# Expert tables with a 512-column moving operand, and the 8 sample tokens' expert rows fetched by indirect DMA

## The reference, cut to what matters

```python
q = (xf @ wq).reshape(n, 8, 2, 128)
s = einsum('nhpd,hpkd->nhpk', q, keys)            # 128 scores for each of 8 heads x 2 halves
top_s, top_i = top_k(s, 16)
best_s, pos = top_k(all 16 x 16 sums, 16)         # 16 of 128 x 128 experts for each head
experts = ...                                     # 8 x 16 = 128 expert numbers for each token
gate = softmax(best_s)
hi = gelu(einsum('bed,bd->be', take(u_tab, experts), x))
y = einsum('be,bed->bd', gate * hi, take(v_tab, experts))
```

## Time and profile before

| | us |
|---|---|
| median of 3 runs | 4418.88 (4409.46 to 4419.07) |
| span of the profiled execution | 4402.0, 16.9 below that median |
| TensorE busy | 4151.5 (94%), weight loads 3973.3 (90%) |
| VectorE, ScalarE, GpSimd busy | 2675.8, 1465.7, 765.7 |
| first table, layer 0 and 1 | 571 to 1546.6 and 2660 to 3628.5 |
| second table, layer 0 and 1 | 1546.6 to 2282.7 and 3628.5 to 4365 |

### The profile page before, as it was taken

How to read it: one execution, slowest core, us unless ns; L and a number is a source line. 1 busy time by engine, 2 the same in 40 slices (tenths; PEclk the granted TensorE clock), 3 DMA queues, 4 the chain that set the end, 5 groups by cost and what they waited for, 6 DMA issues and landing times.

```text
span 4402.0 us, 85855 instructions
## 1 busy us (share of the span) xinstructions
PE 4151.5 (94%) x32404; PEld 3973.3 (90%) x32404; DVE 2675.8 (61%) x5472; ACT 1465.7 (33%) x2084; POOL 765.7 (17%) x430
## 2 busy tenths in 40 slices
PE   8889999999898899999999999999999989999998
PEld 8635899989898899999999789999999889999998
DVE  2332368787786266666653336868787626666665
ACT  3221333434434322222224233433343432222223
POOL 4111123333232300000001012333333320000000
PEclk9989999999999999999999799999999999999999
DMA  4444235766777955555542023576696786555553
GB/s 120 131 128 139 77 113 133 145 132 139 141 139 137 182 183 184 183 184 184 183 134 74 28 77 113 135 144 135 141 147 146 132 174 193 182 182 183 184 184 112
DMA packets 582347, 633.66 MB, mean 144 GB/s; under 512 B 359736, under 2 KB 359864, under 8 KB 581584
## 3 DMA queue, kind: packets, MB, share of 16 engines
q1 hardware_dynamic: 573760, 608.77, 55.0%
q0 software_dynamic: 8464, 23.38, 1.8%
HBM read 491.36 MB, written 140.66 MB: 144 GB/s over the span
## 4 chain that ended last, share of the span: by engine, by line
PE 49%; issue 39%; POOL 8%; ACT 2%; DVE 2%; DMA 1%; POOLq 0%; SPq 0%; ACTq 0%; DVEq 0%
PE aux L1499 33%; PE pstr L1241 9%; POOL wlo L547 8%; PE pstr L1366 1%; PE pstr L1386 1%; PE aux L1284 1%; PE pstr L1339 1%; PE aux L1546 1%; PE aux L1545 0%; PE aux L1275 0%; DVE rstd L847 0%; PE aux L1319 0%; PE aux L1329 0%; ACT xt L604 0%; PE pstr L1275 0%
## 5 line engine op out<-in xcount | busy, mean ns | idle before, releaser
L1241 PE MATMUL pstr<-xh,whi 128*128 128x260 f32 x5504 | 1155.3, 292 | 114.1 <-POOL wlo L547 86.4
L1241 PE MATMUL pstr<-xh,wlo 128*128 128x260 f32 x5504 | 1124.2, 286 | 0.0
L1241 PE MATMUL pstr<-xl,whi 128*128 128x260 f32 x5504 | 1122.6, 286 | 0.0
L1241 PEld LDWEIGHTS pstr<-xh,whi 128*128 128x128 f32 x5504 | 868.7, 193 | 124.8 <-issue 85.5
L547 POOL TENSOR_TENSOR wlo<-wraw,whi 128x1024 fp32r<-128x1024 f32 x252 | 633.4, 2515 | 1460.6 <-ACT whi L570 1459.1
L1241 PEld LDWEIGHTS pstr<-xl,whi 128*128 128x128 f32 x5504 | 867.6, 193 | 0.0
L1241 PEld LDWEIGHTS pstr<-xh,wlo 128*128 128x128 f32 x5504 | 864.9, 192 | 0.0
L1499 PE MATMUL aux<-wth,vhi 128*128 128x260 f32 x4096 | 827.0, 283 | 7.5 <-DVE res L1064 7.5
L1499 PE MATMUL aux<-wth,vlo 128*128 128x260 f32 x4096 | 826.8, 284 | 0.0
L1499 PE MATMUL aux<-wtl,vhi 128*128 128x260 f32 x4096 | 825.5, 283 | 0.0
L1499 PEld LDWEIGHTS aux<-wth,vhi 128*128 128x128 f32 x4096 | 633.4, 189 | 8.5 <-DVE vlo L1043 7.9
(11 more groups left out here) (194 smaller groups left out, 2906.5 us busy)
## 6 DMA issues: line engine op xcount, KB each, us to landing
wraw<-in_u SPq DMA_DIRECT2D x256, 512.0 KB, 3.8
vraw<-in_v SPq DMA_DIRECT2D x512, 256.0 KB, 2.9
hidden<-hid SPq DMA_DIRECT2D x256, 260.0 KB, 2.2
gates<-gst SPq DMA_DIRECT2D x80, 832.0 KB, 18.5
hl<-hidden SPq DMA_DIRECT2D x256, 260.0 KB, 2.7
gc<-gates SPq DMA_DIRECT2D x256, 260.0 KB, 3.9
wraw<-in_w SPq DMA_DIRECT2D x88, 512.0 KB, 3.5
kv<-in_ck SPq DMA_DIRECT2D x32, 256.0 KB, 3.1
```

The source lines that it names most:

```text
L1241: mm = e.matmul(pstr[:, slot, h, 0:HALF], w[:, slot, k * P:(k + 1) * P], x[:, k, h * HALF:(h + 1) * HALF], start=k == 0 and w is whi and x ...
```

## The change

The 512 prompt tokens alone go through the dense tables, as one 512-column matmul in place of two of 260. `hid`, `hidden`, `gates`, `wth`, `wtl`, `gc`, `hl`, `wt` are 512 wide, and the second table uses one bank of `aux` for each block. The last round has 24 gate groups in place of 26; its plan goes from (0, 1, 6) with a tail of 5 pairs to (0, 0, 6) with a tail of 6.

For the 8 sample tokens, in each layer: VectorE makes the list of 128 experts x 8 tokens from `pickt` (`sample_list`). GpSimd waits until all gates are stored and then fetches, one token at a time, its 128 chosen rows of the first table and later of the second (16 indirect DMAs of 128 x 4 KB) into a ring of four buffers. During the first periods of the second table, now written out for groups 0 to 4: TensorE turns the 8 tokens' x into rows (16 transposes, group 0), ScalarE rounds them; in groups 1 and 2 TensorE spreads one token's x over all partitions (4 matmuls of 512 columns) and VectorE multiplies and sums it with the fetched rows (8 times); ScalarE takes Gelu, VectorE multiplies with the gates; in groups 3 and 4 TensorE makes the outputs with the fetched rows as weights and one moving column (64 float32 matmuls), and VectorE adds them to `res` once.

```diff
-PLAN = [(6, 0, 0), (0, 11, 1), (0, 11, 1), (0, 9, 2), (0, 9, 2), (0, 1, 6)]
-TAIL = 5
+PLAN = [(6, 0, 0), (0, 11, 1), (0, 11, 1), (0, 9, 2), (0, 9, 2), (0, 0, 6)]
+TAIL = 6
...
+RING = 4
+DOTS_G, VALS_G = 1, 3
...
@@ store_gates
+                    wide = GH if half < 2 * NT - 1 else LAST_H
@@ gpsimd, end of peer
+                for par in range(2):
+                    e.wait_ge(gates_out[par], 16 * PIECES * NT * (layer + 1))
+                e.wait_ge(s_listed, layer + 1)
+                for j in range(2 * DEC):
+                    table, t = (i["ur"], j) if j < DEC else (i["vr"], j - DEC)
+                    if RING <= j < RING + DEC:
+                        e.wait_ge(s_dot, layer * DEC + j - RING + 1)
+                    elif j >= RING + DEC:
+                        e.wait_ge(s_value, layer * DEC + j - RING - DEC + 1)
+                    e.indirect_dma_start(rows[:, j % RING, :], None, table,
+                                         bass.IndirectOffsetOnAxis(ap=s_id[:, t:t + 1], axis=0)).then_inc(rows_in[j % RING], 16)
@@ vector
+                def sample_dot(t):
+                    e.wait_ge(rows_in[t % RING], 16 * (2 * DEC // RING * layer + t // RING + 1))
+                    e.wait_ge(s_spread, layer * DEC + t + 1)
+                    row = rows[:, t % RING, :]
+                    e.scalar_tensor_tensor(row, row, 1.0, pstr[:, 0, :, :].rearrange("p a n -> p (a n)"), ALU.mult, ALU.mult,
+                                           accum_out=s_dots[:, t:t + 1]).then_inc(s_dot, 1)
...
-                    r = halves(res[:, v, :])
-                    e.tensor_tensor(r, r, aux[:, 2 * (v % 2):2 * (v % 2) + 2, 0:HALF], ALU.add).then_inc(v_taken, 1)
+                    r = res[:, v, 0:SEQ]
+                    e.tensor_tensor(r, r, aux[:, v % 2, :], ALU.add).then_inc(v_taken, 1)
...
+                        if DOTS_G <= g < DOTS_G + 2 and v % 2 == 0:
+                            sample_dot((g - DOTS_G) * 4 + v // 2)
+                        if (g, v) == (VALS_G, 1):
+                            sample_weights()
+                        if (g, v) == (VALS_G + 1, 4):
+                            sample_add()
@@ tensor, chunk
+                        if first in C_U:
+                            mm = e.matmul(pstr[:, slot, 0, :], w[:, slot, k * P:(k + 1) * P], x[:, k, 0:SEQ],
+                                          start=k == 0 and w is whi and x is xh, stop=k == KB - 1 and w is wlo)
+                            continue
@@ tensor, second_table
-                            for h in range(2):
-                                mm = e.matmul(aux[:, 2 * (v % 2) + h, 0:HALF], w[:, v % 4, j * P:(j + 1) * P],
-                                              x[:, par, j, h * HALF:(h + 1) * HALF],
+                            mm = e.matmul(aux[:, v % 2, :], w[:, v % 4, j * P:(j + 1) * P], x[:, par, j, :],
@@ tensor, new
+                def sample_spread(t):
+                    if t == 0:
+                        e.wait_ge(s_rows, 3 * (layer + 1))
+                    if t or layer:
+                        e.wait_ge(s_dot, layer * DEC + t)
+                    for h in range(2):
+                        for n in range(2):
+                            mm = e.matmul(pstr[:, 0, h, :], pickr[:, t:t + 1].to_broadcast([DEC, P]), xr[:, n, h * 512:(h + 1) * 512],
+                                          start=n == 0, stop=n == 1)
+                    mm.then_inc(s_spread, 1)
+                def sample_values(t):
+                    if t == 0:
+                        e.wait_ge(s_weight, layer + 1)
+                    j = DEC + t
+                    e.wait_ge(rows_in[j % RING], 16 * (2 * DEC // RING * layer + j // RING + 1))
+                    for k in range(KB):
+                        at = k * DEC + t
+                        mm = e.matmul(aux[:, 2, at:at + 1], rows[:, j % RING, k * P:(k + 1) * P], s_w[:, t:t + 1], start=True, stop=True)
+                    mm.then_inc(s_value, 1)
```

More of the change, by code:

```diff
@@ L65 @@
 assert (sum(map(sum, PLAN)) + TAIL) * 2 == P and len(PLAN) == NT + 1
-assert all(2 * one + 4 * two == GROUPS for _, one, two in PLAN[1:])
+assert all(2 * one + 4 * two == GROUPS for _, one, two in PLAN[1:-1])
+assert 2 * PLAN[-1][1] + 4 * PLAN[-1][2] == L_GROUPS - (NT - 1) * GROUPS
 NEG = -3.0e38
@@ L217, in trunk @@
         vlo = place("vlo", [P, 4, GROUP * P], F32R)
[L218 to L225, removed]
+        wth = place("wth", [P, 2, GROUP, SEQ], F32R)
+        wtl = place("wtl", [P, 2, GROUP, SEQ], F32R)
+        gc = place("gc", [P, GROUP, SEQ], F32)
+        hl = place("hl", [P, GROUP, SEQ], F32)
+        wt = place("wt", [P, 2, SEQ], F32)
+        rows = place("rows", [P, RING, D_MODEL], F32)
+        xr = place("xr", [DEC, 2, D_MODEL], F32R)
+        pickr = place("pickr", [DEC, DEC], F32R)
+        s_dots = place("s_dots", [P, DEC], F32)
+        s_hid = place("s_hid", [P, DEC], F32)
+        s_w = place("s_w", [P, DEC], F32)
+        assert used[0] <= choice_end, used[0]
+        hid = place("hid", [P, 2, SEQ], F32, choice_end)
+        used[0] = choice_end + 2 * 4 * SEQ + 96
         assert used[0] <= nc.sbuf_usable_end, used[0]
@@ L779, in peer @@
                 hidden_pair(P // 2 - 1)
-                period(0, 0, True)
-                with e.Fori(0, NG // 2 - 1) as q:
+                for g in range(VALS_G + 2):
+                    period(g, g % 2, True)
+                with e.Fori((VALS_G + 1) // 2, NG // 2 - 1) as q:
                     period(q * 2 + 1, 1, True)
@@ L1460, in peer @@
                         pair += zero
[L1461 removed]
+                    n = first_group(tt - 1) if tt else 0
                     if one:
@@ L1506, in period @@
                         second_table(g, v, par)
-                period(0, 0)
-                with e.Fori(0, NG // 2 - 1) as q:
+                        if not isinstance(g, int):
+                            continue
+                        if (g, v) == (0, 4):
+                            sample_turn()
+                        if DOTS_G <= g < DOTS_G + 2 and v % 2 == 0:
+                            sample_spread((g - DOTS_G) * 4 + v // 2)
+                        if g == VALS_G and v >= 2:
+                            sample_values(v - 2)
+                        if g == VALS_G + 1 and v < 2:
+                            sample_values(v + 6)
+                for g in range(VALS_G + 2):
+                    period(g, g % 2)
+                with e.Fori((VALS_G + 1) // 2, NG // 2 - 1) as q:
                     period(q * 2 + 1, 1)
```

74 lines of the change are left out of this document (64 added, 10 removed).

## The result

The changed kernel takes 4453.0 us (median of 4 runs, 4449.02 to 4460.97), the kernel before 4414.17 (4 runs): ratio 1.0102, 95% interval 1.0080 to 1.0124. It is slower by 1.0% (45 us by the ratio; the two medians alone differ by 39), where 4246 was forecast. The profiled execution has a span of 4450.0 against 4402.0.

The account below looks back on a forecast made before the run. TensorE, busy 94% of the span, was taken as the bound. Per layer 73.1 + 40.5 + 1.7 - 29 = 86.3 us, 172.6 for two: span 4229.4, median 16.9 above it, 4246; range 4175 to 4340.

Parts of the forecast that it names:

- the stretch: First table, around a gate store: 44.7 us set by the DMA engines, whose work is nearly unchanged; TensorE's saving becomes waiting.
- best bound: First table: the stalls stay as long as they are and all 128 chunks gain, 73.1 us a layer.
- rival 4: First table: gate stores' stalls don't grow, since part is latency; all 128 chunks gain, 4181 us; chance 0.12.
- the 71 chunks outside the stores: First table: only these chunks gain, 0.571 us each, 40.5 us a layer.
- The count of 5.7 chunks in the 44.7 us: First table: chunks under each of ten gate stores; 57 chunks without gain, 71 with.
- 215.8 ns a matmul: Both tables: time of a 512-column matmul; each replaced pair gives 23.8 ns, 73.1 us a layer in the second table.
- Rival 1: Both tables: the excess beyond the columns stays with each matmul whatever its width; 490 matmuls in 110 us; chance 0.12.
- The 213.3 ns in the range: Both tables: a faster 512-column matmul than the forecast's 215.8 ns; the range's low end, 4175, holds a little of it.
- the samples at 29 us a layer: Cost of the 8 sample tokens' transposes, spreads, value matmuls, dots and fetches: 29 us a layer (16 to 45).
- Rival 5: Sample rows: a fetch takes over 15 us and the rings pace groups 1 to 4; 4310 us; chance 0.06.
- Rival 3: First table: VectorE becomes the bound and the 40.5 us fall away; 4327 us; chance 0.10.
- The slower side: Both tables: float32r stream paced per column at 0.461 ns, a pair gives 3.7 ns; 4438 us; chance 0.09.

Follow-up runs that it names:

- e1: Changed kernel with DRAM rows of `gates` kept at 520 floats (2080 bytes), 512 of them used: 4368.25 us, ratio 0.9908 to the kernel before.
- e4: Changed kernel with 384 of 512 columns in the second table's matmuls and adds (other outputs not updated): 4251.6 us.
- e8: Changed kernel with 64 of 128 weight columns in the second table's matmuls (half the outputs left out): 4430.56 us, 1.015 of the kernel before.
- e6: Changed kernel with `gates` laid out by halves of 52 tokens, stored contiguously and gathered on load: 4200.62 us, ratio 0.9630 to the kernel before.
- e10: e6 with all four inner rounds planned (11,1) and a tail of 4 pairs in place of 6: 4185.37 us, ratio 0.9608 to the kernel before.
- e7: Kernel before with `gates` laid out by half, as in e6: 4265.59 us, ratio 0.9797 to the kernel before.
- e13: e10 with SBUF rows of `xh` and `xl` 544 floats apart in place of 520: 4185.73 us, ratio 0.9500 to the kernel before.
- e5: Kernel before with DRAM rows of `gates` 1024 floats (4096 bytes) apart in place of 520: 4566.1 us, 1.046 of the kernel before.
- e11: Changed kernel with the second table's middle product written to another PSUM bank and not added: 4393.53 us, 1.009 of the kernel before.
- e9: Changed kernel with DRAM rows of `gates` at 528 floats (2112 bytes): 4315.97 us, 0.989 of the kernel before.

## Why the prediction was wrong

The forecast for the span was 4229.4, the result 4450.0: 220.6 us missed, in three terms.

1. **The store of the gates: 89 us.** The step that failed is the sentence that the stretch "is set by the DMA engines, whose work is unchanged but for 1.5% (the 208-byte runs stay)". The runs stayed and their distance did not: 2080 bytes became 2048, because `gates` is listed among the arrays that become 512 wide. The forecast kept the stretch as long as it was, its best bound and rival 4 kept each stall as long as it was; no case had the stalls grow. e1 gives the 89.4 us back by that one edit. The rest of the step held roughly: with the stride restored, the first table gains 12.9 and 3.9 us over before, and what the measured rate would give on the 71 chunks outside the stores is 71 x 0.145 + 1.7 = 12.0. That chunks under a store give nothing fits this, and no more. The count of 5.7 chunks in the 44.7 us is a small slip: it takes the new pace; at the pace of the earlier trace rows, five in 43.5 us, it is 5.2, and the forecast gain would have been 2.9 us a layer more.
2. **215.8 ns a matmul in the second table: 67 us.** It is 226.7, and 3072 x 10.9 = 33.5 us a layer. No run shows the 215.8. It was the author's: 213.3 ns for 512 columns, a figure that no row of the kernel before gives (e4's 0.417 ns a column does), and 2.5 ns beyond them. What the runs showed in its place is 13.3 ns beyond the columns. The forecast took the excess of the 260-column matmul, 119.8 - 260 x 0.417 = 11.5 ns, to go away at 512, with the weight load hidden behind the longer matmul (loads alone follow each other at (1.86 - 0.19) / 15 = 111 ns). That was not shown: it doesn't go away, at 512 columns nor at 384 (e4) nor with half the load (e8). Rival 1, with the chance of 0.12, was that it stays with each matmul whatever its width: 213.3 + 11.5 = 224.8 ns, right in kind and 2 ns short. The row that misled is the float32 one: with twice 0.417 ns a column, its records of 512 and 260 columns have 2 to 3 ns beyond their columns, and that did not carry over to float32r. The forecast took it as the evidence against a fixed cost; it was about another kind of record. The 213.3 ns in the range are the columns alone, and no matmul of 512 columns came nearer to them than 226.7.
3. **The same in the first table: 60 us.** 233.4 in place of 215.8: 17.6 x 24 x 71 = 30.0 us a layer. Of this 10.9 ns a matmul are the same excess and the other 7 no rival had.

89.4 + 67 + 60 = 216 of the 220.6.

What held: the samples at 29 us a layer (30.2 in the second table). Of its parts, TensorE's timeline of the changed kernel shows the spread of one token and a run of its value records, and VectorE's the dot:

```profile
1609.85 1.20 PE L1621 MATMUL pstr<-xr,pickr 8*128 8x512 f32 x4
...
1669.60 1.84 PE L1633 MATMUL aux<-s_w,rows 128*128 128x1 f32 x16
```
```profile
1611.15 1.22 DVE L1104 SCALAR_TENSOR_TENSOR rows<-rows,pstr 128x1024 f32<-128x1024 f32 x1
```

Sixteen records of one column in 1.84 us are the forecast 111 ns, two for each matmul, and the dot took 1.22 us where 1.23 had been read from the earlier trace rows. Rival 5 was wrong: a fetch of 512 KB lands in 5.7 us in the median, 7.0 at most, between the two ends given (3.8 and 6.4, the upper one low by 0.6 at the worst), and the waits for `rows` are GpSimd's alone. Rival 3 was wrong as long as the stores stall: at an undisturbed chunk VectorE waits for TensorE, with 0.43 to 0.59 us left where 0.58 to 0.71 stood in the earlier trace rows, and e6 shows where it becomes true. Rival 4, 4181, is near e10's time, but not by its mechanism: the stalls vanished because the store was rewritten.

The slower side was priced as a cost per column with a chance of 0.09. It came out slower in another way: rival 1, the 7 ns in the first table, and a stride that the forecast had not followed. With the stride kept the change would have been faster by 0.9% (e1), at 4368 us still outside the range, which ended at 4340.

## What to carry to other kernels

When an edit narrows an array, follow it into every DRAM tensor that has that width and read the row stride off: the number of bytes and the size of a run can stay the same and the transfer still get slower, as here at strides of 2048 and 4096 bytes (43.3 and 44.9 ns a packet, where 2080 took 34.2 and 34.8). A short run in one stage is better put on the side of the transfer and at the time where nothing waits: storing contiguously and gathering on load was worth 2% in the kernel before (e7) and over 4% in the changed one (e6), more than the 1.5% of the change itself. Compare absolute times only between kernels that are known not to move, and look at the denominator when a ratio moves (e13). A matmul's cost beyond its columns is read from the same kind of record, or bounded by all of what the present one shows: here, at 0.417 ns a column, the 260-column matmul had 11.5 ns beyond its columns in 119.8, and the 512-column one has 13.3 in 226.7.

## What the runs showed of the hardware

- 208-byte writes to DRAM, mean time of a packet over both layers: 44.9 ns at a stride of 4096 bytes (e5), 43.3 at 2048 (changed kernel; 40.2 in e8, 39.9 in e11), 34.2 and 34.8 at 2080 (before, e1), 32.5 at 2112 (e9); read at the same size, 16.9 ns (e6).
- At a stride of 2048 bytes, the two stores whose runs stay within one 256-byte block of the row take 34.6 to 36.8 ns a packet, the seven that cross 41.1 to 53.8; at 2080, where three runs in four cross, 32.2 to 39.3.
- The kernel with such writes varies by group (before: 4353.19 to 4412.39); the medians of those without agree to 0.4 us.
- A float32r matmul with its own 128 weight columns starts every 173.3 ns at 384 columns (e4) and every 226.7 at 512 (changed kernel; 226.6 with two banks, e11): 0.417 ns a column and 13.3 ns beyond. With 64 weight columns it is 229.8 at 512 (e8), 16.5 beyond. In the first table of the changed kernel it is 233.4, 20 beyond, for no reason that was found.
- An indirect fetch of 128 rows of 4 KB takes GpSimd 0.94 to 1.3 us to issue and lands in 4.4 to 7.0 us (changed kernel).
